# The first modulation third loaded by columns in eight pieces and used two norm rows at a time, in a two-model transformer kernel on one core

## The reference, cut to what matters

```python
s_c, s_cc = silu(c), silu(c_ctx)
mx = s_c @ w_mod[l] + b_mod[l]            # 6 * 1024 columns; mc the same from s_cc
shx1, scx1, gx1, shx2, scx2, gx2 = split(mx, 6)
hx = rms(x, norm1_g[l]) * (1 + scx1) + shx1     # rms: t * rsqrt(mean(t*t) + EPS) * g
hc = rms(ctx, norm1_g[l]) * (1 + scc1) + shc1
p = h @ w_in[l] + b_in[l]                 # the first projection, and then the mixer
```

## Time and profile before

| | |
|---|---|
| median of three runs | 2249.78 us (2249.62 to 2250.47) |
| the profiled execution: its time | 2249.66 us |
| its span in the profile | 2248.0 us |
| PE busy | 2129.2 us, 95% of the span |
| DVE, ACT, POOL busy | 1326.9, 999.8, 375.5 us |
| DMA moved | 310.07 MB, 138 GB/s on average |
| granted TensorE clock, mean over the span | 0.984 |

### The profile page before, as it was taken

How to read it: one execution, slowest core, us unless ns; L and a number is a source line. 1 busy time by engine, 2 the same in 40 slices (tenths; PEclk the granted TensorE clock), 3 DMA queues, 4 the chain that set the end, 5 groups by cost and what they waited for, 6 DMA issues and landing times.

```text
span 2248.0 us, 32786 instructions
## 1 busy us (share of the span) xinstructions
PE 2129.2 (95%) x13220; PEld 1705.8 (76%) x13220; DVE 1326.9 (59%) x2156; ACT 999.8 (44%) x1756; POOL 375.5 (17%) x292
## 2 busy tenths in 40 slices
PE   5999899999999898999999999999999999998999
PEld 3766677878887785899965437787888777648999
DVE  5293657944973665655555334795497455556555
ACT  2434644532542645654553243453254343355443
POOL 1000416512531003100100001651253100000000
PEclk7999899999999999999999999999999999999999
DMA  9553022563457424456534002256344322103564
GB/s 348 196 210 127 20 76 98 194 198 130 169 202 223 126 94 163 151 173 208 169 116 165 1 1 78 92 202 193 113 169 151 119 74 94 57 1 114 178 211 118
DMA packets 264535, 310.07 MB, mean 138 GB/s; under 512 B 5569, under 2 KB 251457, under 8 KB 252097
## 3 DMA queue, kind: packets, MB, share of 16 engines
q1 hardware_dynamic: 259680, 303.33, 40.7%
q10 hardware_dynamic: 4704, 4.65, 0.6%
HBM read 306.91 MB, written 1.05 MB: 137 GB/s over the span
## 4 chain that ended last, share of the span: by engine, by line
PE 76%; DVE 11%; ACT 6%; issue 3%; DMA 2%; POOL 2%; SPq 0%; ACTq 0%; DVEq 0%; POOLq 0%
PE bank L660 75%; DVE weights_low L1748 3%; DVE weights_low L1405 2%; ACT weights_high L2173 1%; DMA modulation_slots<-w_mod 1%; DVE scratch L1397 1%; DVE yT L1397 1%; ACT weights_high L2438 1%; POOL weight_sum L585 1%; PE bank L669 1%; DVE input_low L1397 1%; POOL weights_low L601 0%; DVE scratch L1788 0%; DVE big L1397 0%; ACT L2163 0%
## 5 line engine op out<-in xcount | busy, mean ns | idle before, releaser
L660 PE MATMUL bank<-input_high,weights_high 128*128 128x256 f32 (+1 forms) x2336 | 755.7, 323 | 40.5 <-DVE scratch L1788 16.1
L660 PE MATMUL bank<-input_low,weights_high 128*128 128x256 f32 (+1 forms) x2336 | 738.7, 316 | 0.0
L660 PE MATMUL bank<-input_high,weights_low 128*128 128x256 f32 (+1 forms) x2336 | 737.9, 316 | 0.0
L660 PEld LDWEIGHTS bank<-input_high,weights_high 128*128 128x128 f32 x2336 | 439.5, 188 | 121.0 <-issue 46.2
L1405 DVE TENSOR_TENSOR weights_low<-weight_slots,weights_high 128x1024 fp32r<-128x1024 f32 (+2 forms) x344 | 391.9, 1178 | 217.0 <-ACT weights_high L2173 216.2
L660 PEld LDWEIGHTS bank<-input_high,weights_low 128*128 128x128 f32 x2336 | 439.5, 188 | 34.0
L660 PEld LDWEIGHTS bank<-input_low,weights_high 128*128 128x128 f32 x2336 | 440.0, 188 | 32.2 <-issue 1.0
L2173 ACT ACTIVATE weights_high<-weight_slots 128x1024 fp32r<-128x1024 f32 (+2 forms) x348 | 314.3, 950 | 161.3 <-PE bank L660 148.2
L1748 DVE TENSOR_TENSOR weights_low<-weight_slots,weights_high 128x512 fp32r<-128x512 f32 x216 | 245.9, 1162 | 17.2 <-ACT weights_high L2438 14.6
L660 PE MATMUL bank<-hidden_high,weights_high 128*128 128x256 f32 (+1 forms) x704 | 240.6, 342 | 0.6 <-DVE weights_low L1405 0.4
L660 PE MATMUL bank<-hidden_low,weights_high 128*128 128x256 f32 (+1 forms) x704 | 237.8, 338 | 0.0
(11 more groups left out here) (280 smaller groups left out, 2663.1 us busy)
## 6 DMA issues: line engine op xcount, KB each, us to landing
modulation_slots<-w_mod SPq DMA_DIRECT2D x48, 1024.0 KB, 7.2
modulation_slots<-mod_w SPq DMA_DIRECT2D x48, 1024.0 KB, 6.9
weight_slots<-w_gu SPq DMA_DIRECT2D x44, 1024.0 KB, 5.1
weight_slots<-ffn_w_in SPq DMA_DIRECT2D x44, 1024.0 KB, 5.1
weight_slots<-w_in SPq DMA_DIRECT2D x24, 1024.0 KB, 5.5
weight_slots<-w_down SPq DMA_DIRECT2D x16, 768.0 KB, 4.8
weight_slots<-ffn_w_out SPq DMA_DIRECT2D x16, 768.0 KB, 4.8
weight_slots<-od_w_in SPq DMA_DIRECT2D x12, 1024.0 KB, 5.1
```

Source lines behind the costliest of these rows:

```text
L660: return pe.matmul(o, w, r, start=start, stop=stop, skip_group_check=shared)
```

## The change

The first third (and no other) is loaded in eight pieces of 1 MB by columns: all 1024 rows by 256 columns, so rows of 1 KB. An even piece 2i holds the shifts and an odd one 2i + 1 the scales of the norm rows 2i and 2i + 1. Pieces 0, 1, 6 and 7 lie in the two side slots, 2 to 5 in the big buffer, which is empty at the start, so only pieces 6 and 7 wait for a slot. Behind two pieces the pair of norm rows is complete: PE multiplies a piece with eight matmuls of 256 columns (`first_piece`), ACT copies the bank out (`pair_out`), PE turns it (`first_turn`, four matmuls of two columns against the sum of four pieces of the identity), DVE adds the bias and makes two gains (`first_pair`). Pieces 0 to 3 come before the norm; pieces 4 to 7 and the turns of pairs 2 and 3 are put between the first tiles on PE (`LOADING`), the copies of pairs 2 and 3 into ACT's loop of the norm and their biases and gains into DVE's. The first tiles take both items for each of the rows 0 to 5 (`FIRST_LOADED`). SP's order becomes pieces 0 to 3, items 0 and 1, pieces 4 to 7, item 2, tables, then steps 8 and 9. The squares of the context are made by ACT, after the copy of pair 1, and `high_weights(0)` goes ahead of the root.

```diff
+FIRST_LOADED = tuple((j, k) for k in range(KD - 2) for j in range(2)) + ((0, KD - 2), (0, KD - 1), (1, KD - 2), (1, KD - 1))
+LOADING = {1: ((4,), ()), 2: ((5, 6), ()), 3: ((7,), (2,)), 4: ((), (3,))}
...
-                before = g + 6 if g >= 0 else 2
+                before = g + 6 if g >= 0 else 3
...
+    def piece(self, s):
+
+        room = self.big[:, 4 * s - 4:4 * s, :].rearrange("p a n -> p (a n)") if 2 <= s < 6 else self.side[:, s % SIDES, :]
+        return room.rearrange("p (k c) -> p k c", k=KD)
+
+    def loaded(self, s):
+
+        if 2 <= s < 6:
+            return self.piece_in[s - 2], 16
+        return self.side_filled[s % SIDES], 16 * (s // SIDES - 1 if s >= KD else 1 + s // 6)
...
-        if s >= SIDES:
-            sp.wait_ge(*m.stepped.at(0, s - SIDES))
+        if s >= 6:
+            sp.wait_ge(*m.stepped.at(0, s - (SIDES if s >= KD else 6)))
+        if third == 0:
+            at = D * (s % 2) + 256 * (s // 2)
+            sp.dma_start(m.piece(s), w[:, at:at + 256].rearrange("(k p) c -> p k c", p=P)).then_inc(m.loaded(s)[0], 16)
+            return
...
-    for s in range(SIDES):
+    for s in range(4):
         step(s)
     weights(0)
-    for s in range(SIDES, KD):
+    weights(1)
+    for s in range(4, KD):
         step(s)
-    weights(1)
+    weights(2)
...
-    for g in range(2, len(m.item)):
+    for g in range(3, len(m.item)):
...
-        join_squares(("first", half), t, m.first_squared)
+        join_squares(("first", half), t, m.squared if half else m.first_squared)
...
+    def first_piece(s):
+
+        i, what = divmod(s, 2)
+        pe.wait_ge(*m.loaded(s))
+        if s == 0:
+            pe.wait_ge(*m.conditions.at(0, 1))
+        elif what == 0 and i >= 2:
+            pe.wait_ge(*m.biased.at(0, i - 2))
+        for k in range(KD):
+            j = k % 4
+            o = mm(bank[4 + i % 2][32 * j:32 * j + 32, 256 * what:256 * what + 256], m.cvec[:, k, :], m.piece(s)[:, k, :], k < 4, k >= 4)
+        o.then_inc(m.stepped.sem, 1)
+
+    def first_turn(i):
+        pe.wait_ge(*m.mod_out.at(0, i))
+        for c in range(4):
+            o = mm(bank[4 + i % 2][:, 2 * c:2 * c + 2], m.pair_rows(i)[:, c * P:(c + 1) * P], m.summed[:, :], True, True)
+        o.then_inc(m.mod_turned.sem, 1)
...
-    def first_tiles(items, n, place, ready):
-
-        for j, k in FIRST:
+    def loading(k):
+        pieces, turns = LOADING.get(k, ((), ()))
+        for s in pieces:
+            first_piece(s)
+        for i in turns:
+            first_turn(i)
+
+    def first_tiles(items, n, place, ready, first=False):
+
+        for j, k in FIRST_LOADED if first else FIRST:
+            if first and j == 0:
+                loading(k)
...
+    pe.wait_ge(*m.consts.at(0, 7))
+    for s in range(3):
+        first_piece(s)
+    pe.wait_ge(*m.columns_in.end(0))
     pe.wait_ge(*m.consts.end(0))
-    for k in range(KD):
-        mod_step(k)
-        if k in (4, 6):
-            add_squares(("first", k // 2 - 2), (X, C)[k // 2 - 2], m.first_squared)
-    pe.wait_ge(*m.columns_in.end(0))
-    mod_turn(0)
+    first_turn(0)
+    first_piece(3)
+    add_squares(("first", 0), X, m.first_squared)
+    first_turn(1)
+    add_squares(("first", 1), C)
     keep_busy(6, 8)
...
+    def first_pair(i):
+
+        r = slice(2 * i, 2 * i + 2)
+        dve.wait_ge(*m.mod_turned.at(0, i))
+        o = m.mods[:, 0, :, 0:16].rearrange("p v (s k) -> p s k v", s=2)[:, :, r, :]
+        b = cols[:, L_TAB[0], B_MOD:B_MOD + 16].rearrange("p (s k) -> p s k", s=2)[:, :, r].unsqueeze(3).to_broadcast([P, 2, 2, 2])
+        tt(o, bank[4 + i % 2][:, 0:8].rearrange("p (s k v) -> p s k v", s=2, k=2), b, ALU.add).then_inc(m.biased.sem, 1)
+        dve.wait_ge(*m.biased.at(0, i))
+        for v in range(2):
+            muladd(m.coef[:, 0, v, r], m.mods[:, 0, v, 8 + 2 * i:10 + 2 * i], 1.0, column(L_TAB[0], N1 + 2 * i, 2), ALU.add,
+                   ALU.mult).then_inc(m.gains.sem, 1)
...
+            if L == 0 and which == 0 and i % (2 * per) == 0:
+                if k >= 4:
+                    first_pair(k // 2)
+                dve.wait_ge(*m.gains.at(0, k + 1))
...
-    for half, t in enumerate((X, C)):
-        dve.wait_ge(m.inputs_in[half], 16)
-        for k in range(KD):
-            if k >= 4:
-                dve.wait_ge(*m.square_joined.at(("first", half), max(0, k - 5)))
-            tt(yT[:, 2 + k % 4, t], xT[:, k, t], xT[:, k, t], ALU.mult).then_inc(m.first_squared.sem, 1)
+    dve.wait_ge(m.inputs_in[0], 16)
+    for k in range(KD):
+        if k >= 4:
+            dve.wait_ge(*m.square_joined.at(("first", 0), max(0, k - 5)))
+        tt(yT[:, 2 + k % 4, X], xT[:, k, X], xT[:, k, X], ALU.mult).then_inc(m.first_squared.sem, 1)
+    dve.wait_ge(*m.columns_in.end(0))
+    dve.tensor_reduce(m.summed[:, :], m.ident[:, :].rearrange("p (j r) -> p r j", j=4)[:, 0:2, :], AX.X, ALU.add).then_inc(m.consts.sem, 1)
+    for i in range(2):
+        first_pair(i)
     low_weights(0)
-    dve.wait_ge(*m.columns_in.end(0))
-    bias(0)
-    gains(0, 0)
...
+    def pair_out(i):
+        act.wait_ge(*m.stepped.at(0, 2 * i + 1))
+        F(m.pair_rows(i), bank[4 + i % 2][:, :], ACT.Copy).then_inc(m.mod_out.sem, 1)
...
+            if L == 0 and which == 0 and i == 4 * per:
+                pair_out(2)
+                pair_out(3)
...
     ln_exp_tables()
+    for i in range(2):
+        pair_out(i)
+    act.wait_ge(m.inputs_in[1], 16)
+    for k in range(KD):
+        square(("first", 1), k, C)
+    high_weights(0)
     act.wait_ge(*m.square_added.end(("first", 0)))
     act.wait_ge(*m.square_added.end(("first", 1)))
     rstd("first", slice(0, TOK))
-    high_weights(0)
-    modulate("start", KD - 1)
```

More of the change, by code:

```diff
@@ L338, in mod_bank, with pair_rows, third_at @@
         return self.bank[(4, 5, 4, 5, 4, 5, 4, 4, 4, 5, 4, 5)[third]]
-    def mod_rows(self, third):
-        return self.scr[:, 0:TOK] if third == 0 else self.rs[:, :]
+    def pair_rows(self, i):
+        return self.scr[:, i * TOK:(i + 1) * TOK]
+    def piece(self, s):
[5 more added lines that the diff above has]
+        return self.side_filled[s % SIDES], 16 * (s // SIDES - 1 if s >= KD else 1 + s // 6)
+    def third_at(self, third):
+        return third + PAIRS_OF_ROWS - 1
     def slot_free(self, g):
@@ L407, in signals @@
         self.tables_again = S("tables_loaded_again", (0, 7 * 16), (2, 2 * 16))
+        self.piece_in = [nc.alloc_semaphore(f"modulation_piece_loaded{s}") for s in range(2, 6)]
         self.stored = nc.alloc_semaphore("stored")
@@ L411, in signals @@
         self.tile_done = S("weight_tile_multiplied", (0, self.item[-1].last_tile + 1))
-        self.consts, self.conditions = S("constants_set", (0, 8)), S("conditions_activated", (0, 4))
+        self.consts, self.conditions = S("constants_set", (0, 9)), S("conditions_activated", (0, 4))
         self.params_v, self.lam_exp = S("parameters_derived", (0, 9)), S("lambda_exponents", (0, 2))
[L416 to L419, removed]
+        n = 11 + PAIRS_OF_ROWS
+        self.stepped, self.mod_out, self.mod_turned = S("modulation_steps_multiplied", (0, 96)), S("modulation_rows_out", (0, n)), S(
+            "modulation_turned", (0, n))
+        self.biased, self.gains = S("modulation_biased", (0, n)), S(
+            "norm_gains_made", (0, 2 + 2 * PAIRS_OF_ROWS), (1, 4), (2, 5), (3, 4))
         halves = [("first", half) for half in range(2)]
@@ L423, in signals @@
         kinds = {p: 2 if p == ("ffn", 1) else 1 for p in halves + order}
-        self.first_squared = S("first_squares_made", *((p, KD) for p in halves))
-        self.squared = S("squares_made", *((p, KD * kinds[p]) for p in order))
+        self.first_squared = S("first_squares_made", (halves[0], KD))
+        self.squared = S("squares_made", *((p, KD * kinds[p]) for p in halves[1:] + order))
         self.square_joined, self.square_added = S("squares_joined", *((p, (KD - 2) * n) for p, n in kinds.items())), S(
@@ L679, in mod_step @@
             if third >= 2:
-                pe.wait_ge(*m.biased.at(0, third - (1 if third in (7, 8) else 2)))
+                pe.wait_ge(*m.biased.at(0, m.third_at(third - (1 if third in (7, 8) else 2))))
         for j in range(4):
@@ L686, in mod_turn @@
         picked = ident[:, :].rearrange("p (j r) -> p j r", j=4)[:, :, 0:2]
[L687 to L688 removed]
+        pe.wait_ge(*m.mod_out.at(0, m.third_at(third)))
         for c in range(4):
[L690 removed]
+            i = mm(m.mod_bank(third)[:, 8 * c:8 * c + 8].rearrange("p (j v) -> p j v", j=4), m.rs[:, c * P:(c + 1) * P], picked, True, True)
         i.then_inc(m.mod_turned.sem, 1)
+    def first_piece(s):
+        i, what = divmod(s, 2)
+        pe.wait_ge(*m.loaded(s))
+        if s == 0:
[11 more added lines that the diff above has]
+        o.then_inc(m.mod_turned.sem, 1)
     def modulate(*place):
@@ L1418, in bias @@
         l4, at = third // 3, 16 * (third % 3)
-        dve.wait_ge(*m.mod_turned.at(0, third))
```

(6 more changed lines are left out.)

16 lines of the change are left out of this document (9 added, 7 removed).

## The result

The changed kernel took 2265.61 us (median of four runs, 2263.47 to 2269.34), the kernel before 2249.70 beside it (2246.58 to 2250.47): a ratio of 1.0077, 95% interval 1.0061 to 1.0093. It is slower by 16 us, where 2251.0 had been forecast with a range up to 2255.4. The profiled execution took 2265.01 us with a span of 2263.2 (before 2248.0) and a mean granted clock of 0.987 (before 0.984). I read it in two parts, as the forecast was made: the start, and what lies behind.

What follows compares the result with a forecast made beforehand. It took a chain of waits to bound the start up to the first norm row at 41.61 us, and PE behind it. 2249.66 less 7.0 (earlier norm) plus 8.3 (longer first tiles) gave 2251.0 us; range 2246.9 to 2255.4.

Steps and rivals of the forecast that it cites:

- What lies behind I take to be alike in both kernels: Everything after the first tiles: claimed to take the same time in both kernels, so it added nothing to the sum.
- The stream and the columns: Loads at the start: one stream at 355 GB/s, piece 2 landing near 19.1 us, ACT's queue with the columns by some 17.
- rival 3: Start: columns land at 23.6 us as before, turn 0 starts there, N 2.6 us later, total 2253.5; chance 0.05.
- N: Start of the norm, seen as DVE's first `yT` product: forecast at 34.6 us, 7.0 earlier than before.
- A piece: A piece's matmuls on PE: 1.2 us each between first tiles, 4.8 for four; 1.93 each at the lower clock before N.
- rival 1: Pieces on PE: cost goes by matmuls, eight for four, so up to twice a step; total 2258.4 us, slower; chance 0.13.
- The new wait: First tiles, near 52 us: PE stands 2.5 us for row 3's low halves, queued on DVE behind `first_pair(2)`, which awaits turn 2.
- Rival 5: First tiles: PE's new wait is absent because DVE has row 3's low halves out before; 2.5 us less, 2248.5; chance 0.05.
- Rival 4: First tiles: the clock falls in PE's new wait, slowing the tiles behind it by 2.5 us, total 2253.5; chance 0.06.
- Item 2: End of the first tiles: the low half of item 2 comes slightly after PE needs it, costing 0.2 us.
- The end of the first tiles: PE finishes the first tiles at 69.3 us for 67.96 before, 34.7 us behind N for 26.35.
- the sum for the start: Start through the first tiles: N 7.0 us earlier, then 8.3 us longer to the end of the first tiles.

Runs made afterwards that it cites:

- The earlier start: Changed kernel, arena back, turn 2 behind piece 6, plus: ACT squares context before pair 1's copy, PE sums squares sooner, DVE makes item 0's low halves sooner: 2243.93 us.

## Why the prediction was wrong

The step that failed is one sentence, "What lies behind I take to be alike in both kernels". It stood on the reading that no instruction there is changed, which is so. What was changed is where the operands lie, by an allocation that I did not follow through to the addresses behind it. It measured 12 us of span: 9.4 in two blocks, the rest in shorter ones. The kernel before with 8 unused bytes shows the same loss with nothing else of the change, and the changed kernel with the arena back is free of it. Without it the forecast of 2251.0 stands beside 2252.55. The prediction gave this term nothing, none of the five rivals had the mechanism, and the range ended 10 us short.

The steps of the sum, one by one:

- **The stream and the columns.** 368 GB/s from 5 to 42 us for the 355 taken, without a break, but 276 from 2.5 to 5. Piece 2 was there at 17.80 us for 19.1. The columns landed at 20.38 us, not "by some 17"; between before's 23.6 and that, so rival 3 happened in part. PE stood 0.95 us for them behind piece 2; as that had come early, turn 0 still started at 20.68 for 21.05.
- **N.** 35.19 for 34.6. POOL's six sums took 5.9 us for 4.8 and started 0.5 earlier, and the rest of the chain is as forecast. The mechanism was right, but I took its order as given: the earlier start shows that the order on ACT and PE was 6 us of it.
- **A piece.** 1.20 us between tiles for 1.2, and 1.94 for 1.93 at the lower clock in front of N. Pieces 5 and 6, one right behind the other, cost 2.06 together (44.45 to 46.98 less two matmuls of 0.233). The eight weight loads for four cost nothing, and rival 1 is out: eight matmuls of 256 columns take as long as four of 512.
- **The new wait.** 2.31 us for 2.5, in its place, ended by `input_low`, with DVE idle 8.67 us for "some 9". Moving the turn took it away, which shows what it was waiting for. Rival 5 is out.
- **The clock.** Rival 4 happened beside the forecast, not instead of it. Seven matmuls took 2.98 us (55.31 to 58.29) for 1.63, and the turn behind them 0.97 for 0.88: 1.4 us, where the rival had 2.5. I had weighed it against a wait of 2.8 us that kept the clock and gave it 0.06; here it fell in all three kernels with that wait (0.66 from 55 to 60 us in the changed kernel and in the one with the arena back; 0.75 from 50 to 55 in the one with 32 bytes more), and not in the kernel with only turn 2 moved, which lacks it.
- **Item 2.** 0.28 us for 0.2.
- **The end of the first tiles.** 70.99 for 69.3. N's 0.6, the clock's 1.4 and a turn of 1.05 for 0.88 are 2.2; pieces 5 and 6 side by side and row 0, there 0.3 us sooner behind N than taken, give the rest back.

So the sum for the start was 1.7 us short (+3.0 for +1.3), all of it inside the range. The loss that decided was outside the working altogether.

## What to carry to other kernels

A new buffer is part of a change even if it has 8 bytes: write down the addresses of the operands of the busiest loop before and after, and where they moved, try the change once with the buffer at the end. When a kernel that PE bounds gets slower everywhere by a few per cent at a full clock, compare the same long block of the chain in both traces before looking for a wait; if its count is equal and its time is not, the pace has changed and no queue is to blame. And an operation moved to another engine takes its place in that engine's queue: look at what stands behind it there, as with `sum_of_parts` behind the squares, and then at the order of the engine that waits, as with the context's sum behind turn 1 on PE.

## What the hardware showed that I had not expected

**The pace of a matmul goes by where its operands lie.** At a granted clock of 1.00 and with PE busy throughout, matmuls of 256 columns (`input_high`, `input_low` by `weights_high`, `weights_low`) started between 0.1133 and 0.1200 us apart, steadily over 100 us and more, and those of 512 columns 0.228 to 0.234. The first became up to 3% slower when the arena alone moved by 64 to 192 bytes (0.1166 to 0.1200), and stayed as they were when both moved by 64. The 512-column ones were at 0.228 or 0.229 in all four kernels with `weights_high` on a multiple of 64 bytes and at 0.233 or 0.234 in all others; whether the start of the weights or their distance from the input makes that, the runs don't separate, as the arena always began on such a multiple.

**The placement is not the whole of it.** With the same placement the block of 1332 took 157.56 us in one kernel and 152.02 in two others, and in the kernel with turn 2 moved it took 157.50 where five kernels of the same placement had 156.12 to 156.19, while its block of 1572 was as theirs (184.18):

```profile
933.08 157.50 PE bank L689 x1332
...
2059.01 184.18 PE bank L689 x1572
```

The pace also changes inside a block. In the changed kernel with 32 bytes more, the block begins at 932.15 us with 0.119 us between matmuls (933.75 to 934.70, eight of them), as in the kernel before with the same placement, and by 950 has 0.113, which it keeps for over 100 us. From 950 to 1050 us, first this kernel and then the one before with that placement:

```profile
950.00:1050.00 100.00, 100.00 (x885) 100.00 (x884) 58.54 (x75) 47.55 (x73) 4.45 (x6) 1.00 0.64 200
950.00:1050.00 100.00, 100.00 (x852) 100.00 (x851) 54.75 (x71) 46.27 (x72) 4.45 (x6) 1.00 0.61 190
```

So PE seems to work at one of a few paces for a long while, and the placement decides which there are. That is a guess from one profiled execution of each kernel; it would also explain the wide spread of the changed kernel with 32 bytes more (15 us between its runs). What makes the choice, and which part of the memory or of the weight path is behind it, stays open. The Trainium skill (TensorE: Matmul & The Clock Gate, Wait — 56ns, not 53.3ns?) gives the spacing of matmuls at full clock as the columns over 2.4 GHz and 2.5 ns. That would be 0.109 and 0.216 us here, an estimate from that page; the best measured are 0.113 and 0.228, so the page's figure isn't reached in any of these placements.

**Small rows at the start.** From 2.5 to 5 us, with pieces in rows of 1 KB queued from the first moment, the transfers made 276 GB/s for the 350 later (the kernel before, with steps in rows of 8 KB and one item, made 375 from 2.5 to 5):

```profile
2.50:5.00 2.50, 0.00 (x0) 0.00 (x0) 0.00 (x0) 0.91 (x3) 0.00 (x0) 1.00 0.88 276
22.50:25.00 2.50, 2.50 (x19) 1.14 (x19) 0.41 (x3) 0.56 (x2) 0.00 (x0) 1.00 1.10 350
```

And SP itself is held by issuing them. The first two pieces took it 1.07 us, the next two 6.50 and two items 9.79, so that it was through with item 1 only at 18.2:

```profile
1.84 6.50 SPq L537 DMA_DIRECT2D big<-w_mod  x2
8.38 9.79 SPq L547 DMA_DIRECT2D weight_slots<-w_in  x2
```

The Trainium skill (DMA: Bandwidth & Descriptors, Specifications) has transfers of 512 B and more at line rate; the 1 KB rows measured here, as those in the earlier trace rows, stay below the 435 that 8 KB rows reached in one of those stretches.
